# Order of the first loads on SyncE: split first weights, and weight chunks placed ahead of modulation rows

## Chip, cores and metric

The kernel runs on one core of a Trainium2 chip. The metric is the device time of one execution in microseconds, lower is better. Before the change the median of three runs is 1481.56 us (1479.22 to 1482.02).

## The reference, cut to what matters

A gated MLP layer with a causal mixing of v along the tokens, then a dilated attention layer, then a second block, on 512 tokens of width 1024. The change lies in the first part of the first layer:

```python
shift, scale, gate = ada_mod(c, ada_w, ada_b, 3)     # silu(c) @ w + b, 3 x 1024 values
h = rms_norm(x, norm_g) * (1 + scale) + shift         # 512 x 1024
u, v, z = jnp.split(h @ w_in, 3, axis=-1)             # w_in is 1024 x 6144
u = jax.nn.gelu(u)
v = rms_norm(jax.nn.gelu(v), sgu_g)                   # needs all 2048 columns of v
...
y = u * mixed.reshape(bsz, s, A_WIDTH) * jax.nn.silu(z)
```

All modulation vectors (shift, scale, gate of three norms in the first block, six in the second) are products of one vector with a large matrix.

## The kernel before

The weights of all projections are cut into chunks of 128 partitions x 2048 floats (1 MiB). Chunk w = 2u + par is written `(u, par)` in the code. Chunks 0 to 7 make the 2048 columns of v (256 columns each, all 512 tokens), chunks 8 to 23 make u and z, and so on. Each chunk goes through the same steps: SyncE loads it into `w_raw[par]` (function `load`, L345); ScalarE rounds it to `w_hi[par]` (`to_hi`, L494); VectorE writes the rest, `w_lo[par] = w_raw - w_hi` (`to_lo`, L919), and increments `lo_done`; TensorE waits for `lo_done` (`chunk_ready`) and runs three passes, hi by hi, hi by lo, lo by hi (L1521). There are two buffers of each kind, so that `load` of chunk w waits until `to_lo` of chunk w - 2 is done. In waits, chunks 2, 3, 4, ... count as 1, 2, 3, ... of `lo_done`.

Chunks 0 and 1 are different. They go into `w_first[0]` and `w_first[1]` as plain float32 and are multiplied with `h_full` one channel tile `kt` (128 channels of eight tiles) at a time, as fast as `h_full` comes out: `up_unit` on VectorE multiplies a pair of modulation rows `ada_up` with silu(c) and sums it (two instructions at L912), which gives scale and shift of one tile; ScalarE makes `h_full` from them (L546). The eight loads of `ada_up` (1 MiB each) go through six buffers.

The other modulation vectors are spread over the projections. A unit is one 128 x 1024 tile (512 KiB, one partition per output) that VectorE multiplies with silu(c) and sums (`unit`, L912, which increments `ada_done`). In the v stage there are eight groups of four units, here called row groups g0 to g7, in four buffers `ada_v`. SyncE issues their loads in `ada_v_loads(u, par)`, where group g is (u, par) with g = 2u + par; the load of unit k waits for the unit k - 4, the earlier user of its buffer.

What sets the order is the program text of each engine, by hand; nothing is scheduled. The DMA queue of SyncE serves its transfers in the order of issue. On VectorE the order in the v stage is, and stays: `to_lo(2)`, the eight `h_lo`, g0, `to_lo(3)`, g1, two small things, g2, `to_lo(4)`, g3, `to_lo(5)`, g4, `to_lo(6)`, g5, `to_lo(7)`, g6, `to_lo(8)`, g7, then the statistics of v. So the units that stand between `to_lo(w)` and `to_lo(w + 1)` are, from w = 4 on, those of group g(w - 1).

Of the kernel before, what the change touches and what calls it, by code (L numbers as in the profile page):

```python
# [30 lines left out]
KT = DM // P  # L31
# [15 lines left out]
W_UZ = W_V + 8  # L47
# [64 lines left out]
def program(nc, d):  # L112
# [4 lines left out]
    def at(name, shape, off, dt=F32):  # L117
        return nc.alloc_sbuf_tensor_at(name, shape, dt, offset=off)
# [15 lines left out]
    w_first = [at("w_first0", [P, KT, 256], off_whi[1]), at("w_first1", [P, KT, 256], off_wlo[1])]  # L134
# [117 lines left out]
    def sem(name):  # L252
        return nc.alloc_semaphore(name)
# [9 lines left out]
    w_first_loaded = [sem("w_first_loaded0"), sem("w_first_loaded1")]  # L263
# [48 lines left out]
    def ge(eng, semaphore, value):  # L312

        if not isinstance(value, int) or value > 0:
            eng.wait_ge(semaphore, value)
# [17 lines left out]
    with block:  # L333


        @block.sync
        def _(sp):
            weights, ada_weights = d["weights"], d["ada"]

            def load(u, par, used=2048):  # L340

                src = weights[bass.ds(2 * u + par, 1), :, 0:used].rearrange("a p n -> p (a n)")
                sp.lower_ap_dma(src)
                ge(sp, lo_done, 2 * u + par - 3)
                sp.dma_start(w_raw[par][:, 0:used], src).then_inc(w_loaded[par], 16)  # L345

            def ada_row(k):

                src = ada_weights[bass.ds(k, 1), :, :].rearrange("a p n -> p (a n)")
                sp.lower_ap_dma(src)  # L350
                return src

            def ada_v_loads(u, par):

                for e in range(UNITS_V):
                    k = 2 * UNITS_V * u + UNITS_V * par + e
                    src = ada_row(k)
                    if isinstance(u, int) and k < UNITS_V:
                        sp.wait_ge(up_done, 12)
                    else:  # L360
                        sp.wait_ge(ada_done, k - 3)
                    sp.dma_start(ada_v[e][:, :], src).then_inc(ada_v_loaded[e], 16)

            def ada_loads(u, par):

                for e in range(UNITS_UZ):
                    k = 2 * UNITS_UZ * u + UNITS_UZ * par + e + FIRST_UZ_UNIT
                    src = ada_row(k)
                    if not (isinstance(u, int) and k < FIRST_UZ_UNIT + 2):
                        sp.wait_ge(ada_done, k - 1)  # L370
                    sp.dma_start(ada_raw[e][:, :], src).then_inc(ada_loaded[e], 16)

            def ada_out_loads(u, par):

                for e in range(UNITS_OUT):
                    k = 2 * UNITS_OUT * u + UNITS_OUT * par + e + FIRST_OUT_UNIT
                    src = ada_row(k)
                    if isinstance(u, int) and par == 0:
                        sp.wait_ge(ada_done, FIRST_OUT_UNIT - 1 + min(e, 1))
                        if e == 2:  # L380
                            sp.wait_ge(mix_done, AT)
                    else:
                        sp.wait_ge(ada_done, k - 3)
                    sp.dma_start(ada_out[e][:, :], src).then_inc(ada_out_loaded[e], 16)

            def ada_up_load(kt):

                if kt >= UP:
                    sp.wait_ge(up_done, 2 * (kt - UP) + 2)
                sp.dma_start(ada_up[kt % UP][:, :, :].rearrange("p e k -> p (e k)"), d["ada_first"][kt]).then_inc(ada_up_loaded[kt % UP], 16)  # L390

            sp.dma_start(c_in[:, :], d["c"]).then_inc(c_loaded, 16)
            for half in range(2):
                sp.dma_start(x[:, 4 * half:4 * half + 4, :], d["x"][:, 4 * half:4 * half + 4, :]).then_inc(x_loaded[half], 16)
            sp.dma_start(vecs[:, :], d["vecs"]).then_inc(vecs_loaded, 16)
            ada_up_load(0)
            for par in range(2):
                sp.dma_start(w_first[par][:, :, :].rearrange("p k n -> p (k n)"), weights[par]).then_inc(w_first_loaded[par], 16)
            for kt in range(1, KT):
                ada_up_load(kt)  # L400


            for par in range(2):
                load(1, par)
            for par in range(2):
                ada_v_loads(0, par)
            with sp.Fori(2, W_UZ // 2 + 1) as u:
                for par in range(2):
                    load(u, par)
                    ada_v_loads(u - 1, par)  # L410
            for par in range(2):
                load(W_UZ // 2 + 1, par)
                ada_loads(0, par)
            with sp.Fori(W_UZ // 2 + 2, W_OUTA // 2 + 1) as u:
                for par in range(2):
                    load(u, par)
                    ada_loads(u - W_UZ // 2 - 1, par)
            for par in range(2):
                load(W_OUTA // 2 + 1, par)
                ada_out_loads(0, par)  # L420
            with sp.Fori(W_OUTA // 2 + 2, W_KV // 2 + 1) as u:
                for par in range(2):
                    load(u, par)
                    ada_out_loads(u - W_OUTA // 2 - 1, par)
            with sp.Fori(W_KV // 2 + 1, W_Q2 // 2) as u:
                for par in range(2):
                    load(u, par)
            with sp.Fori(W_Q2 // 2, W_DN2 // 2) as u:
                for par in range(2):
                    load(u, par)  # L430
            for w in range(W_DN2, W_END):
                load(*divmod(w, 2), FF2 * 256)

            for m in range(KT):
                sp.wait_ge(acc_freed, 2 * W_DN2 - 15 + m)
                sp.dma_start(d["out"][:, m, :], x[:, m, :]).then_inc(stored, 16)
            sp.wait_ge(stored, 16 * KT)
# [1081 lines left out]
        def _(pe):  # L1519
            def mm(out, lhsT, rhs, start, stop):  # L1520
                return nc.tensor.matmul(out, lhsT, rhs, start=start, stop=stop)  # L1521
# [111 lines left out]
            pe.wait_ge(csil_ready, 2)  # L1633
            for kt in range(KT):
                pe.wait_ge(hx_done, kt + 1)
                for par in range(2):
                    if kt == 0:
                        pe.wait_ge(w_first_loaded[par], 16)
                    for t in range(TB):
                        last = mm(FIRST_V[par][t][:, 0:256], h_full[:, kt, P * t:P * t + P], w_first[par][:, kt, :], kt == 0, kt == KT - 1)  # L1640
                        if kt == KT - 1 and t % 2 == 1:
                            last.then_inc(mm_done, 1)
# [308 lines left out]
            for t in range(1, 5):  # L1951
# [3 lines left out]
                for u in range(12):  # L1955
                    n = 12 * a + u
# [10 lines left out]
                    if project:  # L1967
                        mi, w = u // 2, w0 + u // 4
                        par = w % 2
# [14 lines left out]
                    if t == 4:  # L1984

                        half = u % 2
# [160 lines left out]
```

## Time and profile before

| | |
|---|---|
| median of the runs | 1481.56 us |
| profiled execution, its own time | 1483.68 us |
| its span in the trace | 1481.9 us |
| TensorE busy | 1457.8 us (98%) |
| VectorE busy | 952.4 us (64%) |
| ScalarE busy | 624.2 us (42%) |
| chain that ended last | 85% TensorE, 7% VectorE, 5% DMA |
| granted TensorE clock, mean | 0.995 |

Times in the trace count from the start of the span. The profiled execution took 1.8 us longer than its span. TensorE is the engine that is almost never idle, so the places that matter are the few where it waits, and the engines whose results come just before they are needed.

### The profile page before, as it was taken

Reading aid. Unit: us, or ns where it says so; the run is one execution under the profiler, and the core shown is the slowest. Engines: PE = TensorE matmul, PEld = TensorE weight load, DVE = VectorE, ACT = ScalarE, POOL = GpSimd, SP = SyncE. Lnnn points to the kernel's source line nnn. Section 1 sums busy time; section 2 is a strip of 40 time slices with the busy share of each in tenths; the row PEclk is TensorE's granted clock in tenths of the full one; section 3 lists DMA queues with packets and bytes.
Section 4 is the critical chain, followed back from the end, with each engine's and each line's share of the span. In section 5 each row is a group of like instructions: output and inputs, shape, how many; then the busy total and the mean of one; then the engine's idle time right before and its main releaser. Section 6 shows DMA issues by size and latency. Waiting matters only on the chain.

```text
span 1481.9 us, 19640 instructions
## 1 busy us (share of the span) xinstructions
PE 1457.8 (98%) x7430; PEld 1190.3 (80%) x7430; DVE 952.4 (64%) x1390; ACT 624.2 (42%) x916; POOL 125.3 (8%) x59
## 2 busy tenths in 40 slices
PE   8999999999999999999999999999899999999999
PEld 6998888888888788888877787777488888888887
DVE  7966776768886566666666768778867343332333
ACT  5734223233465444544533555655545232211221
POOL 0001000001001222222212100000030000000000
PEclk9999999999999999999999999999999999999999
DMA  9984445467512211111101231111031323222222
GB/s 390 357 339 171 171 177 190 187 248 291 227 58 88 83 57 58 58 57 57 57 29 64 78 140 61 57 57 58 0 115 57 114 85 107 91 101 98 85 92 79
DMA packets 34415, 181.09 MB, mean 122 GB/s; under 512 B 3881, under 2 KB 4265, under 8 KB 19762
## 3 DMA queue, kind: packets, MB, share of 16 engines
q1 hardware_dynamic: 32114, 175.22, 31.9%
q10 hardware_dynamic: 2240, 5.04, 0.9%
q8 instruction: 40, 0.66, 0.2%
q14 instruction: 21, 0.17, 0.0%
HBM read 178.14 MB, written 2.11 MB: 122 GB/s over the span
## 4 chain that ended last, share of the span: by engine, by line
PE 85%; DVE 7%; DMA 5%; issue 1%; ACT 1%; SPq 1%; ACTq 0%; DVEq 0%
PE acc L1521 73%; PE ada L1521 4%; PE norm L1521 3%; DMA ada_out<-in_ada 3%; PE turn L1521 2%; DVE w_lo L919 1%; PE turn L1778 1%; PE turn L1897 1%; DMA ada_up<-in_ada_first 1%; DVE ada_up L912 1%; DMA ada_v<-in_ada 1%; DVE ada_out L912 1%; DVE s L912 0%; DVE ada_v L912 0%; DVE h_lo L1075 0%
## 5 line engine op out<-in xcount | busy, mean ns | idle before, releaser
L1521 PE MATMUL acc<-h_hi,w_hi 128*128 128x512 f32 x984 | 401.6, 408 | 0.0
L1521 PE MATMUL acc<-h_hi,w_lo 128*128 128x512 f32 x984 | 384.2, 390 | 0.0
L1521 PE MATMUL acc<-h_lo,w_hi 128*128 128x512 f32 x984 | 384.0, 390 | 0.0
L494 ACT ACTIVATE w_hi<-w_raw 128x2048 fp32r<-128x2048 f32 (+1 forms) x106 | 200.7, 1893 | 119.5 <-PE acc L1521 117.0
L919 DVE TENSOR_TENSOR w_lo<-w_raw,w_hi 128x2048 fp32r<-128x2048 f32 (+1 forms) x89 | 205.9, 2313 | 66.7 <-ACT w_hi L494 66.6
L1521 PEld LDWEIGHTS acc<-h_hi,w_hi 128*128 128x128 f32 x984 | 185.5, 188 | 46.4 <-issue 9.0
L1521 PEld LDWEIGHTS acc<-h_lo,w_hi 128*128 128x128 f32 x984 | 185.5, 189 | 44.5 <-issue 8.1
L1521 PEld LDWEIGHTS acc<-h_hi,w_lo 128*128 128x128 f32 x984 | 184.9, 188 | 39.3
L447 POOL TENSOR_TENSOR w_lo<-w_raw,w_hi 128x2048 fp32r<-128x2048 f32 x17 | 77.3, 4547 | 323.5 <-ACT w_hi L494 323.5
L1521 PE MATMUL acc<-w_hi,h_hi 128*128 128x256 f32 x320 | 92.3, 289 | 0.8 <-DVE w_lo L919 0.8
L1521 PE MATMUL acc<-w_lo,h_hi 128*128 128x256 f32 x320 | 90.2, 283 | 0.0
L1521 PE MATMUL acc<-w_hi,h_lo 128*128 128x256 f32 x320 | 89.3, 283 | 0.0
L912 DVE SCALAR_TENSOR_TENSOR x<-acc,mods,x 128x512 f32<-128x512 f32 (+1 forms) x40 | 33.0, 827 | 82.4 <-PE acc L1521 82.4
L1521 PE MATMUL acc<-gu_hi,w_hi 128*128 128x512 f32 x176 | 68.5, 389 | 0.0
L1521 PE MATMUL acc<-gu_lo,w_hi 128*128 128x512 f32 x176 | 68.5, 389 | 0.0
L1521 PE MATMUL acc<-gu_hi,w_lo 128*128 128x512 f32 x176 | 68.5, 389 | 0.0
L912 DVE SCALAR_TENSOR_TENSOR gu<-tanh_g,acc 128x512 f32<-128x512 f32 x21 | 14.4, 688 | 83.1 <-PE acc L1521 83.0
L912 DVE SCALAR_TENSOR_TENSOR y_half<-norm,y_half 128x512 f32<-128x512 f32 x54 | 37.1, 687 | 46.2 <-ACT y_half L504 46.2
L1521 PEld LDWEIGHTS acc<-w_hi,h_hi 128*128 128x128 f32 x320 | 61.3, 191 | 4.6 <-issue 3.6
L888 ACT ACTIVATE gu_hi<-gu 128x512 f32 (+1 forms) x22 | 13.9, 633 | 117.0 <-DVE gu L912 117.0
L1521 PEld LDWEIGHTS acc<-w_lo,h_hi 128*128 128x128 f32 x320 | 61.3, 192 | 0.5 <-issue 0.5
L1521 PEld LDWEIGHTS acc<-w_hi,h_lo 128*128 128x128 f32 x320 | 60.8, 192 | 0.0
(259 smaller groups left out, 2565.2 us busy)
## 6 DMA issues: line engine op xcount, KB each, us to landing
w_raw<-in_weights SPq DMA_DIRECT2D x102, 1024.0 KB, 4.8
ada_v<-in_ada SPq DMA_DIRECT2D x32, 512.0 KB, 6.3
ada_raw<-in_ada SPq DMA_DIRECT2D x32, 512.0 KB, 5.9
ada_out<-in_ada SPq DMA_DIRECT2D x32, 512.0 KB, 6.3
ada_up<-in_ada_first SPq DMA_DIRECT2D x8, 1024.0 KB, 16.8
w_raw<-in_weights SPq DMA_DIRECT2D x4, 768.0 KB, 4.1
x<-in_x SPq DMA_DIRECT2D x2, 1024.0 KB, 6.2
w_first<-in_weights SPq DMA_DIRECT2D x2, 1024.0 KB, 11.7
```

The source lines that it names most:

```text
L447: nc.gpsimd.tensor_tensor(w_lo[par][:, :], w_raw[par][:, :], w_hi[par][:, :].bitcast(F32), ALU.subtract).then_inc(lo_done, 1)
L494: nc.scalar.activation(w_hi[par][:, 0:used], w_raw[par][:, 0:used], ACT.Copy).then_inc(hi_done, 1)
L888: nc.scalar.activation(gu_hi[:, f, :], gu[par][:, :], ACT.Copy).then_inc(guhi_done, 1)
L912: return nc.vector.scalar_tensor_tensor(out, in0, scalar, in1, op0, op1, **more)
L919: nc.vector.tensor_tensor(w_lo[par][:, 0:used], w_raw[par][:, 0:used], f32(w_hi[par][:, 0:used]), ALU.subtract)\
L1521: return nc.tensor.matmul(out, lhsT, rhs, start=start, stop=stop)
L1778: turned = nc.tensor.transpose(bank, s_b[:, P * b:P * b + P], ident)
L1897: turned = nc.tensor.transpose(T0[:, P * b:P * b + P], s_2[n % 3][:, 0, P * b:P * b + P], ident)
```

## The change

The first weights are loaded as four transfers of 512 KiB in place of two of 1 MiB: first channels 0 to 511 of both chunks, then two `ada_up` loads, then channels 512 to 1023 of both. The semaphore `w_first_loaded` counts by half instead of by chunk, and TensorE waits for it at `kt` = 0 and `kt` = 4. In the v stage each weight chunk's load is issued one row group earlier in SyncE's program. Nothing changes on VectorE, ScalarE or GpSimd, and no transfer is added or left out but for the split.

```diff
+            def first_load(half):
+
+                for par in range(2):
+                    part = slice(1024 * half, 1024 * half + 1024)
+                    sp.dma_start(w_first[par][:, 4 * half:4 * half + 4, :].rearrange("p k n -> p (k n)"), weights[par][:, part])\
+                        .then_inc(w_first_loaded[half], 16)
+
             ada_up_load(0)
-            for par in range(2):
-                sp.dma_start(w_first[par][:, :, :].rearrange("p k n -> p (k n)"), weights[par]).then_inc(w_first_loaded[par], 16)
-            for kt in range(1, KT):
+            first_load(0)
+            for kt in range(1, 3):
+                ada_up_load(kt)
+            first_load(1)
+            for kt in range(3, KT):
                 ada_up_load(kt)


             for par in range(2):
                 load(1, par)
-            for par in range(2):
-                ada_v_loads(0, par)
-            with sp.Fori(2, W_UZ // 2 + 1) as u:
-                for par in range(2):
-                    load(u, par)
-                    ada_v_loads(u - 1, par)
+            ada_v_loads(0, 0)
+            load(2, 0)
+            ada_v_loads(0, 1)
+            with sp.Fori(2, W_UZ // 2) as u:
+                load(u, 1)
+                ada_v_loads(u - 1, 0)
+                load(u + 1, 0)
+                ada_v_loads(u - 1, 1)
+            load(W_UZ // 2, 1)
+            ada_v_loads(W_UZ // 2 - 1, 0)
+            ada_v_loads(W_UZ // 2 - 1, 1)
...
             for kt in range(KT):
                 pe.wait_ge(hx_done, kt + 1)
-                for par in range(2):
-                    if kt == 0:
-                        pe.wait_ge(w_first_loaded[par], 16)
+                if kt % 4 == 0:
+                    pe.wait_ge(w_first_loaded[kt // 4], 32)
+                for par in range(2):
                     for t in range(TB):
```

On SyncE at the start of the program, one piece of the difference (`w_first_58` and `w_first_59` are the buffers of chunks 0 and 1, `ada_up_104` and on those of the first row pairs):

```order
 L395 DMA vecs<-in_vecs 128x175
 L390 DMA ada_up_104<-in_ada_first 128x2048
-L398 DMA w_first_58<-in_weights 128x2048
-L398 DMA w_first_59<-in_weights 128x2048
+L400 DMA w_first_58<-in_weights 128x1024
+L400 DMA w_first_59<-in_weights 128x1024
 L390 DMA ada_up_105<-in_ada_first 128x2048
 L390 DMA ada_up_106<-in_ada_first 128x2048
+L400 DMA w_first_58<-in_weights 128x1024
+L400 DMA w_first_59<-in_weights 128x1024
 L390 DMA ada_up_107<-in_ada_first 128x2048
```

The second and third row pairs now have 1 MiB of first weights ahead of them instead of 2 MiB; all later pairs have as much ahead as before.

On SyncE in the v stage, of before, from the last load of row group g0 over g1 to the first of the loop (`w_raw_52` is `w_raw[0]`, the chunk in that row is chunk 4 in the loop's first pass; `ada_v_110` to `ada_v_113` are the four row buffers):

```order
L362 DMA ada_v_113<-in_ada 128x1024 [waits up_done]
L362 DMA ada_v_110<-in_ada 128x1024 [waits ada_done]
L362 DMA ada_v_111<-in_ada 128x1024 [waits ada_done]
L362 DMA ada_v_112<-in_ada 128x1024 [waits ada_done]
L362 DMA ada_v_113<-in_ada 128x1024 [waits ada_done]
L407 UNCONDITIONAL_BRANCH
L407 ISA
L345 DMA w_raw_52<-in_weights 128x2048 [waits lo_done]
L350 ISA
L362 DMA ada_v_110<-in_ada 128x1024 [waits ada_done]
```

The same stretch of the change (`w_raw_53` is `w_raw[1]`, chunk 5 in the loop's first pass):

```order
L362 DMA ada_v_113<-in_ada 128x1024 [waits up_done]
L345 DMA w_raw_52<-in_weights 128x2048 [waits lo_done]
L362 DMA ada_v_110<-in_ada 128x1024 [waits ada_done]
L362 DMA ada_v_111<-in_ada 128x1024 [waits ada_done]
L362 DMA ada_v_112<-in_ada 128x1024 [waits ada_done]
L362 DMA ada_v_113<-in_ada 128x1024 [waits ada_done]
L417 UNCONDITIONAL_BRANCH
L417 ISA
L345 DMA w_raw_53<-in_weights 128x2048 [waits lo_done]
L350 ISA
L362 DMA ada_v_110<-in_ada 128x1024 [waits ada_done]
```

Before, chunk w was followed by group g(w - 2); now it is followed by g(w - 3): chunk 4 stands ahead of g1, chunk 5 ahead of g2, chunk 6 ahead of g3, and so on to chunk 9 ahead of g6, with g7 behind it. The wait of each load is the one that it had.

## Rows read from the trace of the kernel before

**Rows 1.** The page: span, then busy time, share, count.
```profile
span 1481.9 us, 19640 instructions
PE 1457.8 (98%) x7430; PEld 1190.3 (80%) x7430; DVE 952.4 (64%) x1390; ACT 624.2 (42%) x916; POOL 125.3 (8%) x59
```

**Rows 2.** Waits of TensorE, 0 to 320 us: total, times, longest.
```profile
PE acc L1521 <- DVE w_lo L919: 0.8, 1, 0.8
PE acc L1521 <- ACT h_full L546: 0.4, 1, 0.4
```

**Rows 3.** Chain that ended last, 44 to 72 us: start, length, what.
```profile
54.15 5.83 DMA ada_v<-in_ada
...
61.26 6.32 DMA ada_v<-in_ada
```

**Rows 4.** Timeline of VectorE, opening: start, length, line, what, idle before.
```profile
16.98 1.29 DVE L1069 TENSOR_TENSOR x_n<-x,x_rstd 128x512 f32<-128x512 f32 x2
...
19.01 1.22 DVE L912 SCALAR_TENSOR_TENSOR ada_up<-ada_up,csil 128x1024 f32<-128x1024 f32 x1 [0.74 <-DMA ada_up<-in_ada_first]
...
25.58 1.22 DVE L912 SCALAR_TENSOR_TENSOR ada_up<-ada_up,csil 128x1024 f32<-128x1024 f32 x1
```

**Rows 5.** Timeline of VectorE, 42 to 72 us.
```profile
42.43 2.29 DVE L919 TENSOR_TENSOR w_lo<-w_raw,w_hi 128x2048 fp32r<-128x2048 f32 x1 [0.97 <-ACT w_hi L494]
...
54.18 2.29 DVE L919 TENSOR_TENSOR w_lo<-w_raw,w_hi 128x2048 fp32r<-128x2048 f32 x1
...
63.78 1.23 DVE L912 SCALAR_TENSOR_TENSOR ada_v<-ada_v,csil 128x1024 f32<-128x1024 f32 x1 [1.12 <-DMA ada_v<-in_ada]
...
67.61 1.22 DVE L912 SCALAR_TENSOR_TENSOR ada_v<-ada_v,csil 128x1024 f32<-128x1024 f32 x1
...
68.76 2.28 DVE L919 TENSOR_TENSOR w_lo<-w_raw,w_hi 128x2048 fp32r<-128x2048 f32 x1
```

**Rows 6.** Timeline of SyncE's queue, 50 to 113 us, issues.
```profile
54.77 0.35 SPq L345 DMA_DIRECT2D w_raw<-in_weights  x1
...
65.04 4.16 SPq L362 DMA_DIRECT2D ada_v<-in_ada  x4
71.07 0.33 SPq L345 DMA_DIRECT2D w_raw<-in_weights  x1
...
88.96 0.33 SPq L345 DMA_DIRECT2D w_raw<-in_weights  x1
...
100.49 0.33 SPq L345 DMA_DIRECT2D w_raw<-in_weights  x1
```

**Rows 7.** DMA issues at 100.49 and 105.07 us: KB each, us to landing.
```profile
w_raw<-in_weights SPq DMA_DIRECT2D x1, 1024.0 KB, 4.9
...
ada_v<-in_ada SPq DMA_DIRECT2D x1, 512.0 KB, 5.5
```

**Rows 8.** DMA issues at 93.54 and 50.71 us: KB each, us to landing.
```profile
ada_v<-in_ada SPq DMA_DIRECT2D x1, 512.0 KB, 5.7
...
ada_v<-in_ada SPq DMA_DIRECT2D x1, 512.0 KB, 3.4
```

**Rows 9.** DMA rate in 40 slices of 0 to 240 us.
```profile
GB/s 224 425 429 423 419 421 408 404 163 324 416 413 415 414 368 369 175 378 160 314 3 292 58 329 23 333 20 339 19 339 10 339 23 327 18 333 26 324 45 305
```

**Rows 10.** Timeline of TensorE: first matmuls of chunks 4, 8.
```profile
71.18 0.38 PE L1521 MATMUL acc<-w_hi,h_hi 128*128 128x256 f32 x1 [0.83 <-DVE w_lo L919]
...
117.34 0.40 PE L1521 MATMUL acc<-h_hi,w_hi 128*128 128x512 f32 x1
```

**Rows 11.** Statistics of v and chunk 9: VectorE, ScalarE, chain.
```profile
119.31 0.19 DVE L1097 TENSOR_REDUCE v_stat<-v_sums 128x4 f32<-128x32 f32 x1 [2.75 <-ACT v_sq L576]
...
121.37 1.90 ACT L494 ACTIVATE w_hi<-w_raw 128x2048 fp32r<-128x2048 f32 x1
...
123.30 2.73 DVE L919 TENSOR_TENSOR w_lo<-w_raw,w_hi 128x2048 fp32r<-128x2048 f32 x1 [1.47 <-ACT w_hi L494]
...
129.31 10.90 PE acc L1521 x48
```

## The prediction

> **What bounds the kernel now.** I read the page first: TensorE is busy 1457.8 us of a span of 1481.9 us [rows 1], so only waits of TensorE, or work that becomes late for it, can move the time. Then TensorE's waits up to 320 us, the stretch that the change touches: 0.4 us for `h_full` of channel tile 1, and 0.8 us for `w_lo` of chunk 4 [rows 2]. Then the chain that ended last between 44 and 72 us, to see what makes chunk 4 late: twice the landing of modulation rows, those of g1 and those of g2 [rows 3]. The timelines of VectorE and SyncE's queue show why: the units of g2 start at 63.78, each when its row has landed, the last at 67.61, and `to_lo(4)` stands behind them, from 68.76 to 71.05 [rows 5]. TensorE follows 0.13 us later, at 71.18 [rows 10]. From chunk 4 at 71.18 to chunk 8 at 117.34 TensorE runs without a wait worth counting: 46.16 us for four chunks, 11.54 us each [rows 10].
>
> **The opening.** No operation is added but two more transfer issues on SyncE, far ahead of any use. VectorE waits 0.74 us, until 19.01, for the second pair of `ada_up` rows; before that it is done with `x_n` at 16.98 + 1.29 = 18.27 [rows 4]. The change takes 1 MiB (1.05 MB) from in front of that pair. At the 425 to 429 GB/s of these slices [rows 9] that is 2.4 us, so it lands near 16.5 and the wait goes. Everything on VectorE up to the end of this stage stands back to back and moves forward by 0.74 us. The fourth pair has all 2 MiB in front of it as before: it lands two transfers, 4.9 us, behind the second's old landing of about 19.0, at 23.9, and is wanted at 25.58 - 0.74 = 24.84 [rows 4]. So nothing new is late. The second half of the first weights, one transfer later than the third pair's place, lands near 21.4; TensorE wants it at tile 4, over 10 us after its start on tile 0. On TensorE itself only the 0.4 us are gained [rows 2]. The wait that counts next, chunk 4, hangs on VectorE, so I take 0.74 us.
>
> **Chunks 4 and 5.** Chunk 4 is now loaded as soon as `to_lo(2)` is done (42.43 + 2.29 before, 44.0 now), ahead of g1. But in the queue in front of g2 chunk 5 takes the place of chunk 4: its load waits only for `to_lo(3)`, done at 54.18 + 2.29 = 56.47 before [rows 5] and 55.7 now. Before, chunk 4 was issued at 54.77 [rows 6] while the last row of g1 was still on the way: that row was issued at 54.15 and VectorE got it at 59.98 [rows 3]. So chunk 5 still comes right behind g1, g2 right behind it, and `to_lo(4)` is done at 71.05 - 0.74 = 70.3. TensorE is free at about 69.7 and waits as before. The early load of chunk 4 buys nothing, since `to_lo(4)` stands behind g2 and not behind its own chunk. If the rows of g1 land sooner without the chunk behind them, up to 1.2 us more comes off here: the four rows then follow chunk 5, issued at 55.7, by 4.9 + 4 x 1.25 us, the last at 65.6 instead of 66.9. I take 0, since g1 is as it was.
>
> **Chunks 6 to 9, the large term.** In SyncE's program the rows of g3 now stand behind the load of chunk 6, and that load waits for `to_lo(4)`. Before, g3 stood ahead of it: its rows were issued from 65.04, and chunk 6 at 71.07 [rows 6], so they were landing while VectorE wrote `w_lo` of chunk 4. Now SyncE can't issue g3 before 70.3, and the rows queue behind 1 MiB. VectorE needs g3 at once after `to_lo(4)`, and `to_lo(5)` stands behind g3. When `to_lo(5)` is done, chunk 7 is issued and g4 behind it, and so on: the lead of one row group is gone, and one loop runs through SyncE, the DMA engines and VectorE with nothing overlapped. One turn of it:
> - from the end of `to_lo` to the issue of the chunk, 0.03 us;
> - chunk and four rows, 3 MiB, from an idle queue. The nearest rows are chunk 8 before, issued at 100.49, landing after 4.9 us, and the last of the four rows behind it, issued at 105.07 and landed 5.5 us later, at 110.57 [rows 6, 7]: 10.08 us for the same 3 MiB. There the rows were issued later than they can be now, but the last was still 5.5 us on the way, two more than a lone row (3.4) [rows 8], so it was queued and not late;
> - VectorE's last unit 1.15 us and its hand-over 0.03, then `to_lo` 2.29 us [rows 5].
>
> Sum 13.58 us, against 11.54 us of TensorE. Such turns lie between `to_lo(4)` and `to_lo(5)`, (6), (7) and (8): four. So chunk 8 starts 4 x 13.58 = 54.3 us after chunk 4 and not 46.16 us: +8.2 us. TensorE would wait 2.0 us for each of chunks 5 to 8, and nobody has slack to give there.
>
> A page of the Trainium skill would make this smaller. "DMA: Bandwidth & Descriptors", section "Anatomy of one DMA", puts a transfer at about 2.0 us plus bytes over 436 GB/s; it is stated for another issuing path than SyncE's. By it 3 MiB take 9.2 us, a turn 12.7 us, and the whole change +4.0 us. The chunk issued at 100.49 took 4.9 us where that rule gives 4.4, so the rows here are slower than the rule.
>
> **After chunk 8.** Before, the statistics of v began at 119.31 and chunk 9's `w_hi` at 121.37, 2.06 us later; its `w_lo` was done 4.66 us after that [rows 11]. Now g7's four units (4.6 us) stand between `to_lo(8)` and the statistics. Together 11.3 us after the end of `to_lo(8)`, less if the table load in the 2.06 us is done early; TensorE wants chunk 9 at 129.31 - 117.34 = 11.97 us after it started chunk 8 [rows 10, 11]. So this is hidden by 0.7 us or more. Then the old program goes on, with a TensorE that has no absolute times to meet, and the delay stays.
>
> **Sum.** -0.74 + 8.2 = +7.4 us. On the profiled execution: span 1481.9 to 1489.3 us, its own time 1483.68 to 1491.1. That execution is 2.1 us above the median; I put the difference on the median: 1481.56 + 7.4 = 1489.0 us, 0.5% slower.
>
> **Rivals.**
> - The stream is faster than in the row I took. A lone row landed after 3.4 us [rows 8], of which 1.2 us is its data at 429 GB/s [rows 9], so 2.2 us fixed; 3.15 MB at 429 GB/s are 7.3 us. A turn is then 13.0 us, and the change +5.1 us: 1486.7. For it: the queue is truly idle. Against: the chunk at 100.49 took 4.9 us to land, where this would give 4.6 [rows 7]. With the rule of the page above it would be 1485.6. With g2 early by 1.2 us as well, +3.9. Chance of this group 0.14.
> - A slower turn and a second wait. By the chunk at 88.96 [rows 6], whose last row was issued at 93.54 and landed 5.7 us later [rows 8], a turn's transfers take 10.28 us and the change costs +8.2. If the statistics of v then push chunk 9 beyond its 0.7 us, another 1 to 2 us come on top: up to 1491.8. Chance of this second wait 0.08.
> - Faster, the other side: the loop closes within 11.5 us, so it never shows. Then the opening's 0.74 us and chunk 4's wait of 0.8 us [rows 2] are won: 1480.0. It decides at 8.0 us for 3 MiB from the issue. The data alone takes 7.3 us at the best rate here, and 0.7 us would be left for what takes 2.2 in a lone row. Chance 0.03.
> - The new order does nothing, as the rows' buffers and not their place in the queue hold them back: 1480.8, by the opening alone. Against: g3 was issued at 65.04, 6 us ahead of chunk 6 [rows 6], and its buffers are free from 65 on. Chance 0.03.
>
> **How the numbers follow.** Forecast 0.72, the four rivals 0.14, 0.08, 0.03 and 0.03. The forecast's own bounds are +5.1 to +8.2 us, and a median of three scatters by some 1.5 us to either side. The range goes from +4.0 to +10.0, 1485.6 to 1491.6. A measurement of this kernel can tell about 0.2%, 3 us, from no change. Slower by more: 0.93, since only the corner of the first rival falls under 3 us. Within 0.2%: 0.06. Faster: 0.01.
>
> **What would show it.** In the profile of the changed kernel: the 0.74 us wait of VectorE at 19.01 gone and the first `w_lo` at 41.7; chunk 4 starts at about 70.4; from there TensorE waits some 2 us for `w_lo` four times, at 83.9, 97.5, 111.1 and 124.7; VectorE idles about 6 to 7 us per turn, released by the landing of `ada_v`; the loads of chunks 6 to 9 start within 0.1 us of the end of a `w_lo`, with the four rows close behind; DMA falls idle before each. I am wrong if chunk 8 starts before 119, or if TensorE's waits for `w_lo` come to less than 5 us in all.

## The result and the profile after

The changed kernel takes 1492.72 us (median of four runs, 1488.84 to 1495.1), the kernel before 1481.79 us (1479.22 to 1482.77): ratio 1.0069, 95% interval 1.0049 to 1.0089. The forecast was 1489.0 us with a range up to 1491.6: the right direction and the right place, 3.7 us too little, and 1.1 us outside the range. The interval of the ratio means +7.3 to +13.2 us, with the forecast's +7.4 us at its lower edge, so the size of the miss is read from the traces below. The profiled execution took 1488.84 us and is the fastest of the four.

The page of the changed kernel (span, then busy time, share, count), against [rows 1]:

```profile
span 1487.0 us, 19621 instructions
PE 1457.0 (98%) x7430; PEld 1190.2 (80%) x7430; DVE 951.8 (64%) x1390; ACT 624.1 (42%) x916; POOL 125.3 (8%) x59
```

TensorE does the same work in a span 5.1 us longer. Its waits up to 330 us, against [rows 2]:

```profile
PE acc L1535 <- DVE w_lo L933: 5.6, 3, 3.2
PE acc L1535 <- issue: 3.2, 2, 1.7
```

The wait for `w_lo` was 0.8 us in all and is now 5.6 us in three pieces: 1.95 us before chunk 4, 3.17 before chunk 6, 0.45 before chunk 7. A fourth is filed under "issue", as the next rows show: TensorE begins chunk 8 at 127.67, 0.1 us after `w_lo` is done at 125.29 + 2.29. Chunk 5 has no wait at all; the reason comes below. Its first matmuls of chunks 4 and 8, against [rows 10]:

```profile
72.44 0.38 PE L1535 MATMUL acc<-w_hi,h_hi 128*128 128x256 f32 x1 [1.95 <-DVE w_lo L933]
...
127.67 0.47 PE L1535 MATMUL acc<-h_hi,w_hi 128*128 128x512 f32 x1 [1.75 <-issue]
```

Chunk 4 starts 1.26 us later than before and chunk 8 10.33 us later. The timeline of VectorE between them, the `w_lo` of chunks 4 to 8 and the first units of g3 and g4, against [rows 5]:

```profile
70.01 2.29 DVE L933 TENSOR_TENSOR w_lo<-w_raw,w_hi 128x2048 fp32r<-128x2048 f32 x1
78.37 1.23 DVE L926 SCALAR_TENSOR_TENSOR ada_v<-ada_v,csil 128x1024 f32<-128x1024 f32 x1 [6.07 <-DMA ada_v<-in_ada]
...
83.33 2.29 DVE L933 TENSOR_TENSOR w_lo<-w_raw,w_hi 128x2048 fp32r<-128x2048 f32 x1
93.41 1.23 DVE L926 SCALAR_TENSOR_TENSOR ada_v<-ada_v,csil 128x1024 f32<-128x1024 f32 x1 [7.79 <-DMA ada_v<-in_ada]
...
98.27 2.29 DVE L933 TENSOR_TENSOR w_lo<-w_raw,w_hi 128x2048 fp32r<-128x2048 f32 x1
...
111.75 2.28 DVE L933 TENSOR_TENSOR w_lo<-w_raw,w_hi 128x2048 fp32r<-128x2048 f32 x1
...
125.29 2.29 DVE L933 TENSOR_TENSOR w_lo<-w_raw,w_hi 128x2048 fp32r<-128x2048 f32 x1
```

This is the loop of the forecast: after each `w_lo` VectorE idles 6.1 to 7.8 us until a row lands. The turns, start to start, are 13.32, 14.94, 13.48 and 13.54 us. SyncE's queue over one of them, against [rows 6]:

```profile
72.33 0.33 SPq L345 DMA_DIRECT2D w_raw<-in_weights  x1
72.86 2.08 SPq L362 DMA_DIRECT2D ada_v<-in_ada  x4
```

`w_lo` of chunk 4 ends at 72.30, chunk 6 is issued at 72.33, and the four rows of g3 behind it. Before, g3 was issued from 65.04.

Why do four long turns not give four equal waits of TensorE? The four stretches from the first matmul of one chunk to that of the next, with busy times, then the granted clock of TensorE (1.00 is 2.4 GHz, 0.50 is 1.2 GHz), the DMA share and GB/s:

```profile
72.44:85.75 13.31, 13.25 (x97) 13.05 (x97) 7.14 (x9) 2.93 (x6) 0.00 (x0) 0.87 0.62 236
85.75:100.69 14.94, 11.77 (x97) 11.57 (x97) 7.12 (x9) 7.73 (x17) 0.00 (x0) 0.98 0.55 212
100.69:114.16 13.47, 13.02 (x96) 12.82 (x97) 7.13 (x9) 2.21 (x7) 0.00 (x0) 0.89 0.60 234
114.16:127.67 13.51, 11.77 (x96) 11.59 (x97) 7.24 (x10) 5.99 (x16) 0.00 (x0) 1.00 0.89 333
```

In the kernel before, the same four chunks run at a clock of 1.00. Here the granted clock falls to 0.50 just behind the wait of 1.95 us before chunk 4, and again at the end of that of 3.17 us before chunk 6, each time for about 3.4 us. TensorE then needs 13.0 to 13.3 us for a chunk in place of 11.5 to 11.8, and its work fills most of the turn: the wait has become slower matmuls. The length of a turn is set by VectorE's loop all the same, since TensorE starts each chunk within 0.15 us of the end of its `w_lo`. So the total of the waits, 5.6 us and the 1.75 us under "issue", understates what the loop costs.

### The profile page after: what moved, and what is told of

Read it like the earlier page. It is cut to its first block, busy times and chain, and to the rows that moved or that the text cites. A ratio compares the mean times of both kernels' runs of the same rounds, so it can differ in the third digit from the quotient of the medians.

```text
span 1487.0 us, 19621 instructions
## 1 busy us (share of the span) xinstructions
PE 1457.0 (98%) x7430; PEld 1190.2 (80%) x7430; DVE 951.8 (64%) x1390; ACT 624.1 (42%) x916; POOL 125.3 (8%) x59
## 4 chain that ended last, share of the span: by engine, by line
PE 88%; DVE 5%; DMA 3%; ACT 1%; issue 1%; SPq 1%; ACTq 0%; DVEq 0%
PE acc L1535 77%; PE ada L1535 4%; PE norm L1535 3%; PE turn L1535 2%; DMA ada_v<-in_ada 2%; PE turn L1792 1%; DMA ada_up<-in_ada_first 1%; PE turn L1911 1%; DVE ada_v L926 1%; DVE w_lo L933 1%; DVE ada_up L926 1%; DVE s L926 1%; DVE stat L1389 0%; DVE hx L926 0%; DVE s_b L926 0%
## 5 line engine op out<-in xcount | busy, mean ns | idle before, releaser
L1535 PEld LDWEIGHTS acc<-h_hi,w_hi 128*128 128x128 f32 x984 | 185.2, 188 | 48.2 <-issue 10.9
L1535 PEld LDWEIGHTS acc<-w_hi,h_hi 128*128 128x128 f32 x320 | 62.6, 196 | 10.4 <-issue 10.4
```

## The experiments

One quantity is compared in all of them: the start of chunk 8 on TensorE less the start of the first `x_n` on VectorE, which takes out where the opening began. It is 117.34 - 16.98 = 100.36 us in the kernel before [rows 4, 10] and 127.67 - 17.19 = 110.48 us in the changed one. Columns: that distance, its difference to before, and for the times the median and the ratio with its 95% interval.

| run | x_n to chunk 8 | to before | time, us | ratio |
|---|---|---|---|---|
| changed kernel | 110.48 | +10.1 | 1492.72 | 1.0069 (1.0049 to 1.0089) |
| opening alone | 100.03 | -0.3 | 1482.13 | 0.9997 (0.9984 to 1.0010) |
| v order alone | 110.20 | +9.8 | 1492.47 | 1.0067 (1.0050 to 1.0084) |
| chunk 4 early, lead kept | 99.71 | -0.7 | 1482.73 | 0.9999 (0.9986 to 1.0011) |
| half rows | 99.47 | -0.9 | 1480.59 | 0.9992 (0.9979 to 1.0006) |
| four halves in the old place | 102.04 | +1.7 | 1479.5 (one run) | - |
| second pair ahead of whole weights | 99.63 | -0.7 | 1479.93 | 0.9986 (0.9971 to 1.0001) |
| v order, TensorE's loop written out | 110.93 | +10.6 | 1492.31 | 1.0063 (1.0039 to 1.0087) |
| change's opening, chunk 4 early | 99.98 | -0.4 | 1480.64 | 0.9999 (0.9984 to 1.0014) |
| v order, less beside chunk 4 | 110.24 | +9.9 | 1494.56 (one run) | - |
| second pair first, chunk 4 early | 98.75 | -1.6 | 1480.71 | 0.9990 (0.9976 to 1.0005) |

Differences under 1 us can't be told in the second column. With the opening as before, VectorE waits for the second row pair until about 19.0 whenever `x_n` began: 0.25 to 1.06 us in the five traces that have it, and this wait is part of the distance.

### Either half of the change by itself

The opening of the change with the old v stage:

```diff
             ada_up_load(0)
-            for par in range(2):
-                sp.dma_start(w_first[par]...)
+            first_load(0)
...
+            first_load(1)
```

> Only the opening of the change: the first weights in halves with two row pairs between, the v stage as before. Theory (the order of the v stage makes the whole loss): the wait of VectorE for the second row pair is gone, but the fourth pair comes late, as in the changed kernel (0.58 us of waiting at 25.6), so that little is won: within 1 us of the kernel before, chunk 8 starts at 117.3 +- 0.8. Rival (the half transfers cost DMA time that is missing later): slower than before by 2 us or more, chunk 4 and chunk 8 start 2 us later than before (73.2 and 119.3).

No difference in time, and chunk 8 starts at 116.53. VectorE waits 0.81 us for the fourth pair, which is late as expected. The rival is out: nothing is missing later. The other half:

```diff
...
-            with sp.Fori(2, W_UZ // 2 + 1) as u:
-                for par in range(2):
-                    load(u, par)
-                    ada_v_loads(u - 1, par)
+            with sp.Fori(2, W_UZ // 2) as u:
+                load(u, 1)
+                ada_v_loads(u - 1, 0)
+                load(u + 1, 0)
+                ada_v_loads(u - 1, 1)
...
```

> Only the new order of the v stage: chunk w's load ahead of row group g(w - 3), the opening as before. Theory: all of the loss is here, +9 to +11 us, and chunk 8 starts at 126.5 to 128; a turn from one w_lo of chunks 4 to 8 to the next takes 13.3 to 13.6 us, one of them near 15 where an instruction fetch runs in the same turn. Rival (part of the loss comes from the split halves): +8 us or less, chunk 4 starts at 71.2 as before and not at 72.4.

The whole loss is here, 1.0067 against 1.0069. Turns of 13.37, 14.86, 13.45 and 13.52 us. Chunk 4 starts at 71.67, half a microsecond later than before although the first `w_lo` was 0.2 us earlier: neither 71.2 nor 72.4, so the order alone makes g2 late too.

### Is it the lost lead, or the early chunk?

```diff
-            for par in range(2):
-                ada_v_loads(0, par)
-            with sp.Fori(2, W_UZ // 2 + 1) as u:
-                for par in range(2):
-                    load(u, par)
-                    ada_v_loads(u - 1, par)
+            ada_v_loads(0, 0)
+            load(2, 0)
+            ada_v_loads(0, 1)
+            ada_v_loads(1, 0)
+            with sp.Fori(2, W_UZ // 2) as u:
+                load(u, 1)
+                ada_v_loads(u - 1, 1)
+                load(u + 1, 0)
+                ada_v_loads(u, 0)
...
```

> Opening as before. In the v stage only chunk 4's load moves ahead of row group g1, and g2 follows g1 directly; from chunk 5 on the order is that of before, with g3 behind chunk 5 and so on, so that the lead of one row group stays. Theory (the loss is the lost lead, not the early chunk): no loop, TensorE's 0.8 us wait for w_lo of chunk 4 goes since nothing of 1 MiB stands ahead of g2, chunk 8 starts at 116.5, 0.8 us faster than before, at most within 1 us of it. Rival (the early chunk 4 load beside ScalarE's transfers is what makes g2 late): chunk 4 starts at 72 or later as in the changed kernel, +1 us or more.

The loop is gone with the lead kept, and the early chunk does no harm. TensorE's waits for `w_lo` are gone altogether; chunk 8 starts at 116.21. Timeline of VectorE of this run, g2's third unit and `w_lo` of chunk 4:

```profile
64.96 1.22 DVE L917 SCALAR_TENSOR_TENSOR ada_v<-ada_v,csil 128x1024 f32<-128x1024 f32 x1 [0.25 <-DMA ada_v<-in_ada]
...
67.46 2.29 DVE L924 TENSOR_TENSOR w_lo<-w_raw,w_hi 128x2048 fp32r<-128x2048 f32 x1
```

`to_lo(4)` starts 1.3 us earlier than in [rows 5]. Chunk 4 moved ahead of g1 is worth that only if chunk 5 stays behind g2. In the time it does not show: 0.9999.

### Is it bytes around a loop?

```diff
-                    sp.dma_start(ada_v[e][:, :], src).then_inc(ada_v_loaded[e], 16)
+                    sp.dma_start(ada_v[e][:, 0:512], src[:, 0:512]).then_inc(ada_v_loaded[e], 16)
```

with `unit` on 512 columns for these rows. The kernel leaves out half of each of these sums.

> The changed kernel, but each row load and each unit of the v stage takes 512 of 1024 columns (half of each of these sums is left out). A turn then moves 2 MiB: about 4.9 + 4 x 0.62 us, the last unit 0.6 and to_lo 2.3, in sum some 10.4 us, under TensorE's 11.54. Theory (one loop through SyncE, DMA and VectorE longer than TensorE's chunk): the waits of TensorE for w_lo from chunk 5 on are gone, chunk 8 starts at 116.5 to 117.5, the time is 1480 to 1482.5. Rival (SyncE's place or the number of transfers, not their bytes, makes the waits): waits of 1 us or more per chunk remain and the time stays above 1485.

With the same order, waits and number of transfers, TensorE's waits for `w_lo` are gone, and the time is that of before. But the turns are 12.51, 12.03, 11.66 and 11.04 us and not the 10.4 I expected: the first row's unit still starts 5.7 to 7.7 us after `w_lo` is done. They sum to 47.2 us, 1.1 more than TensorE's 46.16, and don't show because `w_lo` of chunk 4 is done at 65.03 + 2.29 = 67.3, over 2 us before TensorE is free. So less work on the rows takes away most of a turn's excess, and not all of it. The edit halves the units too: of the 2.0 us that a turn lost on the mean, about 0.5 us are the last unit, which takes 0.6 us in place of 1.15. The time is won in two places, the shorter turns and the earlier chunk 4.

### Why the opening gave nothing

The change's first half transfers, put back in one place:

```diff
             ada_up_load(0)
-            for par in range(2):
-                sp.dma_start(w_first[par]...)
+            first_load(0)
+            first_load(1)
```

> The kernel before, but the first weights as four transfers of 512 KiB one behind the other in their old place (both first halves, then both second halves), no row pair between, v stage as before. Theory (the half transfers themselves run slower: in the changed kernel and in the run with the opening alone the DMA rate falls to 190 GB/s near 12 us, where the first halves move): the rate dips again near 12 us by about 1 us in all, the second row pair lands at 19.8 to 20.2 instead of 18.8 to 19.0, and VectorE waits 1.5 us or more for it. Rival (the dip comes from the row pair that moves beside them): no dip, the second pair lands at 18.9 as before.

The dip is there with no row pair between, and the second pair is late: VectorE waits 2.37 us, until 20.02. The row pair beside the halves is not the cause. Rates in 40 slices of 5 to 30 us and the bytes of that stretch, of the kernel before, of the changed kernel and of this run:

```profile
GB/s 419 433 433 419 358 467 419 433 419 446 446 419 419 433 419 419 433 420 419 433 446 419 419 419 419 433 419 419 419 433 419 433 406 433 419 419 419 419 419 419
DMA packets 1587, 10.60 MB, mean 424 GB/s; under 512 B 176, under 2 KB 304, under 8 KB 304
```

```profile
GB/s 393 419 419 419 364 455 439 433 413 387 341 190 321 367 406 400 426 419 419 419 446 426 400 413 413 439 452 426 452 419 419 419 419 419 433 419 419 419 419 419
DMA packets 1827, 10.22 MB, mean 409 GB/s; under 512 B 207, under 2 KB 335, under 8 KB 847
```

```profile
GB/s 419 433 419 419 382 483 446 433 400 328 249 210 302 400 406 426 420 419 452 459 433 419 420 419 433 433 420 446 419 433 419 419 419 419 419 433 419 419 419 419
DMA packets 1831, 10.24 MB, mean 410 GB/s; under 512 B 208, under 2 KB 336, under 8 KB 848
```

The first halves, two transfers of 128 x 4 KiB out of rows of 8 KiB, fall to 190 to 210 GB/s; the stretch moves 0.38 MB less, 0.9 us at 424 GB/s. The second halves barely dip. Why the first ones do was not found. The other way to bring the second pair forward keeps the transfers whole:

```diff
             ada_up_load(0)
+            ada_up_load(1)
             for par in range(2):
                 sp.dma_start(w_first[par]...)
-            for kt in range(1, KT):
+            for kt in range(2, KT):
```

> The kernel before, but the second row pair's load is issued ahead of the first weights, which stay two whole transfers of 1 MiB. Theory (whole transfers do not dip): the rate stays at 419 to 433 GB/s, VectorE has no wait for the second pair and none for the fourth, the first weights land 2.4 us later, near 18.7, so that TensorE starts its first float32 chunk at 18.7 to 19.0 instead of 18.2 to 18.6; the first w_lo starts 0.6 to 0.7 us earlier against x_n than before (before: 42.43 - 16.98 = 25.45, here 24.8), chunk 8 starts 0.5 to 0.8 us earlier, the time is within 1.5 us of before. Rival (later pairs come late whatever is in front): a wait of 0.5 us or more for the fourth pair, the first w_lo not earlier.

No dip, no wait for either pair, and from `x_n` to the first `w_lo` 41.48 - 16.77 = 24.71 us against 25.45 before: the 0.74 us that I had forecast for the change. In other executions it is worth 0.25 to 1.06 us, as long as the wait that it removes. TensorE started at 18.41, so the whole weights were in time.

### Why one turn is longer

```diff
-            with pe.Fori(2, W_UZ // 2) as u:
-                v_pair(u)
+            for u in range(2, W_UZ // 2):
+                v_pair(u)
```

> The run with the new v order alone, but TensorE's loop over chunks 4 to 7 is written out, so that its instructions are fetched for chunks 6 and 7 too. Theory (the turn of 14.9 us is long because the fetch of 16 KB over one of the DMA engines near 88 us holds up the transfers of that turn): a second and perhaps a third fetch fall in the turns that end near 112 and 127, and at least one of these grows from 13.5 to 14.2 to 15 us; chunk 8 starts 0.7 to 2.5 us later than 126.8. Rival (the long turn has another cause, such as the loop of SyncE or VectorE taking its first branch back): the turns stay at 13.4, 14.9, 13.5, 13.5.

The turns are 13.31, 14.87, 14.96 and 13.42 us: one more is long. DMA queues of this run from 108 to 111 us (packets, MB, share of 16 engines):

```profile
q1 hardware_dynamic: 125, 0.44, 36.1%
q8 instruction: 1, 0.02, 2.2%
```

The queue that brings instructions has one packet there, between 109 and 110 us, and from 97 to 112 us it has none in the changed kernel. Such a packet has 16 KB: over the whole changed kernel this queue has 40 packets and 0.66 MB. The turn that ends at 112.47 is the one that grew by 1.5 us, and its last row came 1.42 us late:

```profile
108.67 1.23 DVE L917 SCALAR_TENSOR_TENSOR ada_v<-ada_v,csil 128x1024 f32<-128x1024 f32 x1
111.32 1.23 DVE L917 SCALAR_TENSOR_TENSOR ada_v<-ada_v,csil 128x1024 f32<-128x1024 f32 x1 [1.42 <-DMA ada_v<-in_ada]
112.47 2.29 DVE L924 TENSOR_TENSOR w_lo<-w_raw,w_hi 128x2048 fp32r<-128x2048 f32 x1
```

In the second turn of the four runs with the new order and full rows such a packet stands between 84 and 93 us, and the chunk of that turn lands after 6.2 to 6.3 us instead of 4.7 to 4.9. Counted from the first `w_lo` chunk 8 starts 1.4 us later than in the run with the v order alone (128.28 - 42.31 against 126.84 - 42.23). A further packet, near 125 us, comes when the rows of its turn have landed, and costs nothing. In the run with half rows such packets fall into the two longest turns, near 67 and 85 us; the third turn has none and still took 11.66 us. The 1.4 us do not show in the times, 1492.31 against 1492.47 us; they scatter by more.

### The remaining lateness of chunk 4, and the best order

ScalarE's 512 KiB load of `b_sp` taken away from beside chunk 4's early load and issued at the end of the v stage:

```diff
-            act.dma_start(b_sp...).then_inc(small_loaded, 16)
...
+            act.dma_start(b_sp...).then_inc(b_sp_loaded, 16)
```

> The run with the new v order alone, but ScalarE's 512 KiB load of b_sp, which used to run beside chunk 4's early load between 45 and 52 us, is issued at the end of the v stage. Rival for why g2 is late (the early chunk shares the DMA engines with ScalarE's transfers and leaves one of them behind): g2's first unit starts 0.6 us or more earlier against the first w_lo than in that run (64.29 - 42.23 = 22.06, so 21.4 or less), chunk 4 at 71.0. Other theory (g2 is late because chunk 5 can only be issued at the end of to_lo(3), 1.9 us later than chunk 4 was in that place before, and lands late for itself): the distance stays at 21.9 to 22.2 and chunk 4 starts at 71.5 +- 0.3. The four turns behind are 13.4, 14.9, 13.5, 13.5 by both.

From the first `w_lo` to g2's first unit it is 64.71 - 42.50 = 22.2 us: the rival is out. Chunk 5 is issued at 56.42, and g2's first unit starts 8.3 us later. The single time of this run says nothing more, since VectorE later waits 2.10 us for `b_sp`. Last, both orders that gained:

```diff
             ada_up_load(0)
+            ada_up_load(1)
...
+            ada_v_loads(0, 0)
+            load(2, 0)
+            ada_v_loads(0, 1)
+            ada_v_loads(1, 0)
...
```

> Both pieces that gained in a trace: the second row pair ahead of the whole first weights, and chunk 4 early with the lead of one row group kept. Theory: no wait of VectorE for the second or fourth pair, none of TensorE for chunk 4; the first w_lo starts at 41.3 to 41.6, chunk 8 at 115.3 to 115.8, 1.5 to 2 us before the kernel before; time 1480 +- 1.5, ratio 0.998 to 0.9995, at the edge of what can be told. Rival (the gain at chunk 4 is already used up by the opening): chunk 8 at 116.3 or later, ratio 1.000.

Chunk 8 starts at 115.98, or 1.6 us earlier counted from `x_n`: 0.7 us up to the first `w_lo` and 0.9 us behind it. By the times it can't be told from the kernel before. The change's own opening with chunk 4 early gives less:

> The opening of the change together with chunk 4 early and the lead of one row group kept. Theory: both gains add where they don't share a wait: VectorE's first w_lo as in the changed kernel, no wait of TensorE for chunk 4, chunk 8 starts at 115.7 to 116.4, 1.0 to 1.6 us before the kernel before, the time 0.05 to 0.1% under it, too little to be told by the times. Rival (the early chunk 4 spoils the row groups when the opening is changed too): chunk 4 waits 0.5 us or more, chunk 8 at 117 or later.

Chunk 8 at 116.31, but TensorE still waits 0.3 us for `w_lo` of chunk 4, so by the traces the whole transfers are the better opening. The times can't tell the two (1480.64 and 1480.71 us).

## Why the prediction was right in kind and short in size

| step of the prediction | forecast | measured |
|---|---|---|
| first `w_lo` against before | -0.74 us | +0.05 us |
| `to_lo(4)` done | 70.3 | 72.30 |
| its end to that of `to_lo(8)`, four turns | 54.3 us | 55.28 us |
| after chunk 8 | nothing added | nothing added |
| chunk 8 against before | +7.4 us | +10.3 us |

**The opening (wrong).** The failed step is "The fourth pair ... lands ... at 23.9, and is wanted at ... 24.84". I had priced the halves at the rate of whole transfers. The fourth pair's load, its landing (KB each, us from issue), and VectorE's first use of the second and of the fourth pair in the changed kernel:

```profile
6.61 0.48 SPq L390 DMA_DIRECT2D ada_up<-in_ada_first  x1
ada_up<-in_ada_first SPq DMA_DIRECT2D x1, 1024.0 KB, 19.0
18.40 1.22 DVE L926 SCALAR_TENSOR_TENSOR ada_up<-ada_up,csil 128x1024 f32<-128x1024 f32 x1
...
25.63 1.22 DVE L926 SCALAR_TENSOR_TENSOR ada_up<-ada_up,csil 128x1024 f32<-128x1024 f32 x1 [0.58 <-DMA ada_up<-in_ada_first]
```

The fourth pair landed at 6.61 + 19.0 = 25.6, 1.7 us later than forecast. The dip accounts for 0.9 us of it and a queue that was 0.2 us late from the first pair on for a little more; the rest was not traced. VectorE started on it at 25.63 and before at 25.58 [rows 4]. Everything behind is that 0.05 us later, and nothing of the 0.74 us is left. The run with four halves in one place shows the cost, and the one with whole transfers shows that the 0.74 us were to be had.

**Chunk 4 (wrong).** I wrote that chunk 5 "still comes right behind g1" and so `to_lo(4)` at 70.3. Of the 2.0 us that this missed, 0.8 us are the opening's. The other 1.2 us are g2: chunk 5 can't be issued before `to_lo(3)` is done, at 56.63, where chunk 4 had been issued at 54.77 [rows 6], and it landed 7.2 us after its issue. The run with the v order alone has it too. Sharing with ScalarE's load of `b_sp` is excluded. Chunk 5's issue on SyncE and g2's first unit on VectorE in the changed kernel:

```profile
56.63 0.35 SPq L345 DMA_DIRECT2D w_raw<-in_weights  x1
65.13 1.23 DVE L926 SCALAR_TENSOR_TENSOR ada_v<-ada_v,csil 128x1024 f32<-128x1024 f32 x1 [2.52 <-DMA ada_v<-in_ada]
```

The first unit of g2 starts 8.0 to 8.5 us after chunk 5's issue, and that of a turn from an idle queue 6.0 to 6.3 us after the chunk's. The queue was not idle here. The bytes moved from chunk 5's issue to 72 us, of the changed kernel and of the run with the v order alone:

```profile
DMA packets 903, 3.79 MB, mean 247 GB/s; under 512 B 109, under 2 KB 109, under 8 KB 774
DMA packets 957, 4.00 MB, mean 255 GB/s; under 512 B 112, under 2 KB 112, under 8 KB 828
```

Chunk 5 and the four rows of g2 are 3.15 MB of these. The other 0.64 and 0.85 MB are mostly what was left of g1, and at the 384 to 388 GB/s of this stretch they take 1.7 and 2.2 us, about the 1.7 to 2.5 us that are to be explained. No run takes them away, so this is a reading of the traces and not shown by a change.

**The loop (right, 1.0 us short).** Three turns measured 13.3 to 13.5 us for 13.58. The row that I took, 10.08 us for 3 MiB, held. "TensorE would wait 2.0 us for each of chunks 5 to 8" did not: the waits were 0, 3.17, 0.45 and 1.75 us, as the clock at 0.50 took up the wait of chunk 5 and most of that of chunk 7. The fourth was 14.9 us, as an instruction fetch held up that turn's transfers. Before, the same fetch cost TensorE nothing: the rows had slack. The rule of the page "DMA: Bandwidth & Descriptors", section "Anatomy of one DMA", in the Trainium skill would have made a turn 12.7 us (an estimate); the turns of 13.3 us and more decide for the rows. That the loop makes the loss is shown from three sides: the order alone costs all of it, the kept lead nothing, and with half rows the turns fit beside TensorE's work.

**After chunk 8 (right).** GpSimd's second staging of v starts at 129.50 before and 139.90 after, the same 10.4 us as at chunk 8.

**Of the rivals**, the faster stream did not come. The second wait behind chunk 8 did not come either. The new order was not without effect, and the loop did not close within 11.5 us. The range did not follow from its own terms: +5.1 and +8.2 us with 1.5 us to either side are +3.6 to +9.7, not +4.0 to +10.0. Its upper end had room for neither a late chunk 4 nor a costly opening.

**From chunk 8 to the time.** The profiled span grew by 5.1 us only, while the other three runs of the changed kernel lie 10.9 to 13.3 us above the median of before. GpSimd's rows at the start and at the end of the stage between 790 and 1100 us tell where 3.0 us of the difference go; of the kernel before, then of the changed kernel:

```profile
792.78 0.95 POOL L479 MEMSET wf_hi<- 128x1024 f32 x1 [4.25 <-PE ada L1521]
...
1089.20 1.75 POOL L461 TENSOR_TENSOR sq_sum<-sq,sq 128x512 f32<-128x512 f32 x1 [262.36 <-ACT sq L527]
```

```profile
802.47 0.95 POOL L493 MEMSET wf_hi<- 128x1024 f32 x1 [4.23 <-PE ada L1535]
...
1095.93 1.75 POOL L475 TENSOR_TENSOR sq_sum<-sq,sq 128x512 f32<-128x512 f32 x1 [259.42 <-ACT sq L541]
```

The stage took 296.42 us in the one and 293.46 us in the other, and the code of it is the same. The delay is 9.7 us when it begins and 6.7 us when it ends. What differs is TensorE's granted clock. Three stretches of the kernel before, with busy times, granted clock, DMA share and GB/s:

```profile
1052.00:1056.00 4.00, 4.00 (x15) 2.41 (x17) 2.74 (x6) 3.21 (x6) 0.00 (x0) 0.57 0.02 4
1069.00:1073.00 4.00, 4.00 (x22) 3.06 (x23) 3.57 (x8) 1.41 (x3) 0.00 (x0) 0.57 0.00 0
1127.00:1131.00 4.00, 4.00 (x12) 3.14 (x11) 3.90 (x7) 1.87 (x3) 0.00 (x0) 0.57 0.00 0
```

Each holds about 3.4 us at 0.50, two in this stage and one in the last, while the changed kernel's execution has 1.00 in both stages. At half the clock 3.4 us hold 1.7 us of work at the full one, so each can cost up to 1.7 us, an estimate: the two in this stage go with its 3.0 us, the one behind it with the 1.6 us that the delay loses in the last stage, from 6.7 to 5.1. The 0.6 us lost before 793 were not traced. So this pair of executions hides 4.6 us of a delay that the kernel has, by the luck of the clock. The changed kernel's mean granted clock is 0.996 in the profiled execution and 0.993 or 0.994 in the other three, which fits their longer times; no trace shows where they lost it.

## What to carry to other kernels

When a load that waits for a result is moved ahead of other loads in one queue, everything behind it waits for that result too. Ask who needs those, and whether the result after next stands behind them: if so, the move closes a loop, and its length is the sum of transfers and compute with no overlap. A transfer split in two can cost more than the whole; look at the rate in the slices where it moves. Move a load ahead of others only if its own wait is over before theirs. And don't add up an engine's waits to price a loop: here TensorE's slower matmuls at a clock of 0.50 hid part of them. Compare when the same piece of work starts instead.

## What was not expected of the hardware

- Half transfers of 128 x 4 KiB out of 8 KiB rows ran at 190 to 210 GB/s for a moment at the first two and at nearly full rate at the next two, in every run that had them, where whole rows ran at 419 to 446 GB/s.
- One packet of instructions, 16 KB, in the middle of transfers that VectorE waits for cost 1.4 to 1.5 us, more than the packet's share of the bytes.
- The stage between 790 and 1100 us takes one of two times, whichever kernel it is. It took 293.4 us in the eight traces where the granted TensorE clock has no stretch below 1.00 in it (changed kernel, opening alone, v order alone and five others). It took 296.3 to 296.4 us in the four with two stretches at 0.50 (kernel before, chunk 4 early, the run with less beside chunk 4 and the last order). A single execution can't tell 3 us here.
- At waits of TensorE of 1.95 and 3.17 us the granted clock fell from 1.00 to 0.50 for about 3.4 us; after the wait of 1.50 us before chunk 4 in the run with the v order alone it stayed at 1.00. In the stage above, the kernel before has waits of 1.7 to 1.9 us ahead of its two falls near 1052 and 1069 us; the changed kernel has waits of 1.7 and 1.9 us at the same places and no fall.
